# New timetables for three mixers, an early mean in the layer norms, and a block norm whose squares TensorE sums

## The reference

```
first block, twice:                                   # alpha = 4 ** 0.25
    x = layer_norm(alpha * x + 0.5 * swiglu_ffn(x))    # "ffn1", 2816 wide
    x = layer_norm(alpha * x + hybrid_mixer(x))        # "mixer"
    x = layer_norm(alpha * x + 0.5 * swiglu_ffn(x))    # "ffn2"
second block, with 16 meta tokens ahead of the 512:
    h = h + 0.5 * swiglu(rmsnorm(h))
    h = h + [diff_attention | top-k latent attention](rmsnorm(h) @ w_in) @ w_out
    h = h + 0.5 * swiglu(rmsnorm(h))
```

## Time and profile before

| | before |
|---|---|
| median of 3 runs | 3179.1 us |
| the profiled execution | 3178.52 us, span 3177.1 us |
| mean granted TensorE clock | 0.987 |
| PE busy | 3067.3 us, 97% |
| DVE busy | 1416.9 us, 45% |
| ACT busy | 1179.3 us, 37% |
| POOL busy | 372.4 us, 12% |
| DMA queues | 26% of 16 engines' span, 269.62 MB |

### The profile page before, as it was taken

One profiled execution on the slowest core, in us unless ns is written; L12 is line 12 of the kernel. 1 busy time (PEld: TensorE's weight loads), 2 busy tenths in 40 slices (PEclk: granted clock), 3 DMA queues, 4 the chain that ended last, 5 costly groups with the idle time before them and its releaser, 6 DMA issues.

```text
span 3177.1 us, 39372 instructions
## 1 busy us (share of the span) xinstructions
PE 3067.3 (97%) x16470; PEld 2564.3 (81%) x16470; DVE 1416.9 (45%) x2118; ACT 1179.3 (37%) x1914; POOL 372.4 (12%) x275
## 2 busy tenths in 40 slices
PE   9999999999999999999999999999999789799999
PEld 7888876888888888886788888899998657688888
DVE  3332455643335333375573333644323666554432
ACT  3322366433214222265552222522223456442321
POOL 0000133300001000033310001100014122110000
PEclk9999999999999999999999999999999899899999
DMA  4223221232232323331222233222233101122232
GB/s 157 93 92 92 97 87 54 67 107 93 91 97 78 107 93 89 97 108 54 67 81 99 93 91 95 69 91 91 84 93 108 34 27 41 34 87 93 98 88 80
DMA packets 76496, 269.62 MB, mean 85 GB/s; under 512 B 8720, under 2 KB 9008, under 8 KB 76064
## 3 DMA queue, kind: packets, MB, share of 16 engines
q1 hardware_dynamic: 74448, 260.08, 25.4%
q0 software_dynamic: 1872, 7.04, 0.7%
HBM read 264.97 MB, written 2.11 MB: 84 GB/s over the span
## 4 chain that ended last, share of the span: by engine, by line
PE 88%; DVE 6%; ACT 4%; issue 1%; DMA 0%; POOL 0%; SPq 0%; DVEq 0%; ACTq 0%
PE psum L339 25%; PE psum L342 24%; PE psum L345 24%; PE psum L400 3%; PE psum L412 2%; PE psum L362 1%; PE psum L358 1%; PE psum L360 1%; PE psum L636 1%; ACT w_hi L284 1%; DVE x_lo L703 1%; PE psum L2599 1%; DVE b_rank L2874 1%; ACT prob L1729 0%; DVE x L788 0%
## 5 line engine op out<-in xcount | busy, mean ns | idle before, releaser
L295 DVE TENSOR_TENSOR w_lo<-w_raw,w_hi 128x1024 fp32r<-128x1024 f32 (+1 forms) x442 | 551.5, 1250 | 1246.7 <-ACT w_hi L284 1246.6
L339 PE MATMUL psum<-x_hi,w_hi 128*128 128x512 f32 (+1 forms) x2792 | 967.9, 371 | 8.6 <-ACT neg_mean L2670 5.2
L342 PE MATMUL psum<-x_hi,w_lo 128*128 128x512 f32 (+1 forms) x2792 | 951.1, 365 | 0.0
L345 PE MATMUL psum<-x_lo,w_hi 128*128 128x512 f32 (+1 forms) x2792 | 946.3, 363 | 0.0
L284 ACT CAST w_hi<-w_raw 128x1024 fp32r<-128x1024 f32 (+1 forms) x490 | 504.0, 1029 | 1170.9 <-PE psum L345 1134.3
L339 PEld LDWEIGHTS psum<-x_hi,w_hi 128*128 128x128 f32 x2792 | 503.2, 190 | 114.2 <-issue 16.8
L342 PEld LDWEIGHTS psum<-x_hi,w_lo 128*128 128x128 f32 x2792 | 502.4, 190 | 87.7 <-issue 5.7
L345 PEld LDWEIGHTS psum<-x_lo,w_hi 128*128 128x128 f32 x2792 | 503.0, 190 | 84.4
L339 PE MATMUL psum<-h_hi_ffn,w_hi 128*128 128x512 f32 (+1 forms) x792 | 296.9, 375 | 0.0
L342 PE MATMUL psum<-h_hi_ffn,w_lo 128*128 128x512 f32 (+1 forms) x792 | 292.2, 369 | 0.0
L345 PE MATMUL psum<-h_lo_ffn,w_hi 128*128 128x512 f32 (+1 forms) x792 | 290.7, 367 | 0.0
(11 more groups left out here) (384 smaller groups left out, 3440.9 us busy)
## 6 DMA issues: line engine op xcount, KB each, us to landing
w_raw<-in_ffn_gu SPq DMA_DIRECT2D x176, 512.0 KB, 3.2
w_raw<-in_ffn_down SPq DMA_DIRECT2D x64, 512.0 KB, 3.5
w_raw<-in_w_in SPq DMA_DIRECT2D x44, 512.0 KB, 3.3
w_raw<-in_b_gate SPq DMA_DIRECT2D x44, 512.0 KB, 3.2
w_raw<-in_b_up SPq DMA_DIRECT2D x44, 512.0 KB, 3.3
w_raw<-in_b_down SPq DMA_DIRECT2D x32, 512.0 KB, 3.5
w_raw<-in_ffn_down SPq DMA_DIRECT2D x32, 384.0 KB, 3.1
w_raw<-in_b_in SPq DMA_DIRECT2D x24, 512.0 KB, 3.3
```

The lines of the kernel that those rows point to most:

```text
L295: nc.vector.tensor_tensor(w_lo[s][:, 0:n], w_raw[r][:, 0:n], w_hi[s][:, 0:n].bitcast(F32), ALU.subtract).then_inc(*w_low_dve.inc(u))
L339: nc.tensor.matmul(out, w_h, hi[:, c], start=first and i == 0, stop=False)
L342: nc.tensor.matmul(out, w_l, hi[:, c], start=False, stop=False)
L345: done = nc.tensor.matmul(out, w_h, lo[:, c], start=False, stop=final and i == n - 1)
```

## The change

- The start times and lags of the mixers' steps become tables (`TIMES_1`, `LAGS_1`, `TIMES_2`, `LAGS_2`), with other values. Steps hang on a start by a lag, as before. A lag can be negative.
- The mean that a layer norm shifts by is now that of two feature tiles of the old `x` (0 and 1), scaled. POOL adds the two (`pool_pair`), TensorE sums over features (`pe_mean`), ACT negates, and DVE makes x = scale * x - mean for all 8 tiles (`dve_shift`). In a feed-forward stage this happens at up-steps 20 (TensorE), 22 (ACT) and 24 to 38 (DVE); in a mixer at 19.9 to 24.3. The results of the product are then added without a scale. In the feed-forward norm POOL sums 7 tiles instead of 6, ACT squares each tile as it comes, and the sums and squares on POOL take turns.
- In the block norm TensorE sums the squares, one sum for each tile and part (`pe_square`), in three rotating buffers; POOL has no part in it. `x_hi` is made at once from the scaled tile, with the bias folded in (`shift2`), before `x` itself. The meta tokens' part (`act_meta`, `dve_meta`, 8 small matmuls) moves into the feed-forward stage before. The mean is copied to SBUF, and `dve_centre` reads it there.
- Small moves: `MixNorm`'s sums of part 1 one step later in `pe_group`, two weight splits on ACT earlier.

```diff
-EARLY = 6
 OUT_PAIRS = KT // 2
+
+
+
+TIMES_1 = {'turned': [0.38, 0, 0, 0.65, 0, 0.01, 0.1, 0, 0.07, 0.57, 0.36, 0.69, 0.17],
+ 'v_made': [2.53, 0.62, 0.26, 0.86, 1.58],
+ 'items': [6.34, 7.06, 8.68, 9.66, 12.97, 13.72, 16.16, 17.1],
+ 'retention': [9.28, 12.43, 15.67, 18.77],
+ 'r_high': 25.22,
+ 'mean': 20.2,
+ 'shift': [20.35, 20.57, 21.18, 21.19, 21.38, 23.27, 23.68, 24.26]}
+LAGS_1 = {'turned': [('swap', 0.41), ('cosine', 0.42), ('sine', 0.45), ('turned', 0.77)],
+ 'value': [('v_raw', -0.09), ('v_turn', 0.46)],
+ 'item': [('score', -0.02), ('mask', -0.0), ('exp', 0.56), ('denom', 1.15), ('prob', 1.22),
+          ('turn', 2.24), ('p_made', 2.56), ('value', 3.0), ('y_high', 3.06), ('y_low', 3.17)],
+ 'retention': [('weighted', 0.78), ('r_score', 0.87), ('k_turn', 0.88), ('k_made', 0.89),
+               ('decay', 0.9), ('r_kv', 1.08), ('state', 1.09), ('r_out', 1.63), ('o_made', 2.05),
+               ('r_sum', 2.1), ('o_centred', 2.28), ('o_square', 2.33), ('r_stat', 2.73),
+               ('o_root', 2.88), ('o_inverse', 2.89), ('o_norm', 2.94)],
+ 'mean': [('pair', -0.31), ('mean', -0.14), ('negate', 0.05)]}
+TIMES_2 = {'a': [9.64, 10.49, 11.1, 12.3, 12.63, 13.42, 14.35, 14.75, 21.6, 21.84, 22.63, 23.45, 24.58,
+       24.86, 25.79, 26.12],
+ 'b': [16.73, 17.1, 17.51, 17.88, 18.26, 18.59, 19.11, 19.28, 19.91, 20.33, 20.76, 21.05, 21.42,
+       21.85, 22.31, 23.13],
+ 'dots': [5.75, 5.9, 6.3, 6.48, 7.97, 8.08, 9.01, 9.12, 12.01, 12.23, 12.89, 13.07, 16.86, 17.03,
+          17.65, 17.74],
+ 'rounds': [(7.25, 0.102), (9.76, 0.281), (14.36, 0.31), (18.22, 0.265)],
+ 'window': [1.92, 3.15, 4.2, 5.32],
+ 'v_b': [1.22, 1.54, 1.93, 2.03, 2.17],
+ 'lat': [0.33, 0.45],
+ 'o': [3.55, 1.19, 1.42, 1.31],
+ 'a_y': [24.97, 24.49, 23.19, 25.69],
+ 'b_y': [23.81, 23.83, 23.83, 24.25],
+ 'first': 25.03}
+LAGS_2 = {'q_i': [('q_i', -0.39)],
+ 'k_i': [('k_i', 0.35)],
+ 'w_i': [('w_raw', -0.4), ('w_turn', -0.09), ('w_made', -0.08)],
+ 'q': [('q_square', -0.02), ('q_stat', 0.21), ('q_root', 0.35), ('q_inverse', 0.36)],
+ 'k': [('k_square', -0.21), ('k_stat', 0.58), ('k_root', 0.59), ('k_norm', 0.84)],
+ 'v': [('v_raw', 0.15), ('v_turn', 0.22), ('v_made', 0.23)],
+ 'c': [('c_add', 0.26), ('c_stat', 0.84), ('c_root', 0.85), ('c_norm', 1.02)],
+ 'v_b': [('v_b', 0.29), ('v_b_made', 0.48)],
+ 'qb': [('qb_raw', -0.18), ('lat_add', 0.64), ('lat_stat', 0.7), ('lat_root', 0.82),
+        ('lat_inverse', 0.86)],
+ 'lat': [('lat', -0.16), ('lat_square', 0.08)],
+ 'window': [('flip', -0.8), ('window', -0.27)],
+ 'dots': [('dots', 0.03), ('relu', 0.09), ('accumulate', 0.16)],
+ 'a': [('a_score', 0.07), ('a_bias', 0.09), ('a_exp', 0.39), ('a_mix', 0.49), ('a_turn', 0.79),
+       ('a_copy', 0.84), ('a_value', 1.04), ('a_out', 1.12)],
+ 'a_y': [('a_y_turn', 0.44), ('a_y_high', 0.54), ('a_y_low', 0.73)],
+ 'b': [('b_score', -0.04), ('b_mask', 0.06), ('b_bias', 0.12), ('b_top', 0.37), ('b_exp', 0.5),
+       ('b_turn', 0.7), ('b_inverse', 0.71), ('b_copy', 0.82), ('b_value', 1.01),
+       ('b_out', 1.02)],
+ 'b_y': [('b_y_turn', 0.03), ('b_y_high', 0.15), ('b_y_low', 0.16)]}
...
+                    if leave.first_mean and i == 20:
+                        leave.pe_first_mean()
...
+                    if leave.before_block and s == 12:
+                        leave.act_meta()
+                    if leave.first_mean and s == 22:
+                        leave.act_first_mean()
...
+                    if leave.before_block and s == 15:
+                        leave.dve_meta()
+                    if leave.first_mean and 24 <= s < 24 + 2 * KT and s % 2 == 0:
+                        leave.dve_shift((s - 24) // 2)
...
+            def pool_pair(self):
+                pool.wait_ge(*self.x_before(0))
+                pool.wait_ge(*self.x_before(1))
+                nc.gpsimd.tensor_tensor(neg_mean[:, TOK], x[:, 0, TOK], x[:, 1, TOK],
+                                        ALU.add).then_inc(*self.paired.inc(0))
+
+            def pe_mean(self, out):
+                pe.wait_ge(*self.paired.at(0))
+                nc.tensor.matmul(out, ones[:], neg_mean[:, TOK], start=True,
+                                 stop=True).then_inc(*self.mean_summed.inc(0))
+
+            def act_negate(self, product):
+                act.wait_ge(*self.mean_summed.at(0))
+                nc.scalar.mul(neg_mean[:, TOK], product,
+                              -self.scale / (2 * P)).then_inc(*self.negated.inc(0))
+
+            def dve_shift(self, m):
+                dve.wait_ge(*self.negated.at(0))
+                dve.wait_ge(*self.x_before(m))
+                if m < 2:
+                    dve.wait_ge(*self.paired.at(0))
+                nc.vector.scalar_tensor_tensor(
+                    x[:, m, TOK], x[:, m, TOK], self.scale, neg_mean[:, TOK],
+                    ALU.mult, ALU.add).then_inc(*self.shifted.inc(m))
...
+            def pe_begin(self):
+                pe.wait_ge(*self.first.meta_low.at(KT - 1))
+
+            def pe_square(self, k, part):
+                if k == 0:
+                    pe.wait_ge(*self.first.mean_copied.at(part))
+                pe.wait_ge(*self.first.sq2.at((k, part)))
+                done = self.first.pe_sum(256, self.squares[k % 3], part, k == 0, k == KT - 1)
+                done.then_inc(*self.first.sq2_summed.inc((k, part)))
+
+            def pe_within(self, part, step):
+
+                if (part, step) == (0, 1):
                     self.first.pe_late(1)
-                if (part, k) == (1, 9):
-                    self.first.pe_rms(0)
-                if (part, k) == (2, 0):
-                    self.first.pe_rms(1)
+                k = step if step < 2 else step - 2
+                if part < 2 and step not in (2, 3):
+                    if k:
+                        self.pe_square(k - 1, part)
+                    elif part:
+                        self.pe_square(KT - 1, 0)
+                if (part, step) == (2, 0):
+                    self.pe_square(KT - 1, 1)
+
...
+            def dve_centre(self, k, part):
+                c = self.cols[part]
+                dve.wait_ge(*self.inverse.at(part))
+                dve.wait_ge(*self.mean_copied.at(part))
+                nc.vector.tensor_tensor(x[:, k, c], x[:, k, c], neg_mean[:, c],
+                                        ALU.add).then_inc(*self.centred.inc((k, part)))
 
             def act_out(self, k, part):
 
-                c, full = self.cols[part], self.spread(part)
+                c, second = self.cols[part], self.second
                 act.wait_ge(*self.scaled.at((k, part)))
+                nc.scalar.activation(x_hi[:, k, c], x[:, k, c], ACT.Identity,
+                                     bias=shift2[:, k:k + 1], scale=gain(second.g, k)).then_inc(
+                                         *second.high.inc((k, part)))
                 nc.scalar.activation(x[:, k, c], x[:, k, c], ACT.Identity,
                                      bias=gain(self.b, k)).then_inc(*self.moved.inc((k, part)))
+                if k >= 3:
+                    act.wait_ge(*self.sq2_summed.at((k - 3, part)))
                 act.wait_ge(*self.moved.at((k, part)))
-                nc.scalar.mul(x_hi[:, k, full], x[:, k, full], gain(self.second.g, k)).then_inc(
-                    *self.second.high.inc((k, part)))
-                if k >= 3:
-                    act.wait_ge(*self.total2.at((k - 2, part)))
-                nc.scalar.activation((square[k % 2] if k else sq_sum)[:, full], x[:, k, full],
+                nc.scalar.activation(second.squares[k % 3][:, c], x[:, k, c],
                                      ACT.Square).then_inc(*self.sq2.inc((k, part)))
 
...
             def end_dve(self):
-                for m in range(2):
-                    self.dve_shift(m)
                 for m in range(KT):
-                    if m + 2 < KT:
-                        self.dve_shift(m + 2)
+                    self.dve_second(m, 0)
                     if m == 1:
                         dve_split(self.u_second + OUT_PAIRS - 1)
-                    self.dve_second(m, 0)
                 dve_split(self.u_next)
                 self.dve_second(0, 1)
...
-            item_start = [6.2, 7.1, 8.0, 9.2, 11.0, 13.0, 15.2, 17.3]
...
             wide = lambda tile: tile in kind and kind[tile][0] in wide_kinds
             ended = lambda tile: GROUP + 0.04 * tile if tile < GROUP else tile + 1.0
             a_items = [(h, b) for h in range(A_HEADS) for b in range(NB)]
-            a_start = [9.7, 10.7, 11.7, 12.7, 13.2, 13.9, 14.6, 15.3,
-                       21.6, 22.2, 22.8, 23.4, 24.55, 25.15, 25.8, 26.45]
+            a_start, dots_at, rounds_at = TIMES_2["a"], TIMES_2["dots"], TIMES_2["rounds"]
             b_items = [(b, h) for h in range(B_HEADS) for b in range(3)] + \
                 [(3, h) for h in range(B_HEADS)]
-            b_start = [16.4 + 0.4 * i for i in range(12)] + [21.2 + 0.5 * i for i in range(4)]
-            dots_at = [6.5, 9.0, 12.2, 16.0]
```

(25 more changed lines are left out.)

324 lines of the change are left out of this document (138 added, 186 removed).

## The result

The changed kernel takes 3132.01 us (median of 4 runs, 3129.83 to 3134.31) against 3178.89 for the one before beside it. The ratio is 0.9852, with a 95% interval of 0.9839 to 0.9864; the forecast was 3131. The profiled execution took 3134.31 us with a span of 3132.6, 44.5 less than before.

A forecast was written before the change was run, and what follows sets the result against it. TensorE, busy 3067.3 of 3177.1 us, was taken as the bound, so only its stalls and low-clock stretches could give time. Last mixer -37, first two -10, block norm -1: -48 on 3178.5, forecast 3131, range 3092 to 3169.

The forecast's parts named there:

- The last mixer's lists: Last mixer: new step order ends TensorE's stalls and clock dips; -20 us net idle, -17 clock, sum -37, bounds +8 and -75.
- The new waits: Last mixer: waits that the new list creates elsewhere, between 0 and 31 us, taken as 7.
- +4 for the uncovered 12 steps: Last mixer's end: `b_turn` 15 to `a_y_turn` 1 run with no product to cover them; costs 0 to 8 us, taken as 4.
- leaves 2: Last mixer's tail: waits of 3.3 us at `a_turn` 14 and 2.9 at `b_turn` 15, with `first` 3 put between, leave 2.
- the clock's part: Last mixer: of 23 us lost to the lowered clock about 17 go, as dips follow the long waits that vanish.
- The first two mixers: First two mixers' new lists: 3.2 us of waits and 1.8 of clock go, 5 each, 10 for two; bounds 0 and 26.
- The shifts: End of the first two mixers: moving eight shifts off VectorE's last stretch gains 0 us; the 4.8 us wait stays.
- The block norm: Block norm: squares summed on TensorE, GpSimd's adds gone; -1 us in the sum, bounds -3 and +7.
- The 14 sums: Block norm: 14 more sums on TensorE, 6.0 us, all but about 1 us covered; if nothing were, +6.0.
- The stalls move: Rival, last mixer: VectorE becomes the bound in the dense stretch and the dips stay; -20 us, 3159, chance 0.19.
- Slower: Rival, last mixer: early `k_square` and `qb_raw` steps hold up ScalarE and long waits return; +10 us, 3189, chance 0.07.
- the sign that I gave for it: Last mixer: it decides where ScalarE's idle time in front of the early steps exceeds a quarter of product, 1.39 us.

The follow-up runs named there:

- ksq_late: The kernel after, with the four k_square steps back from -0.21 to +0.03 of a tile behind their product; 3136.70 us, ratio 0.9865.
- early_mean_only: The kernel before with the early mean of two feature tiles alone, old lists and old block norm; 3181.26 us, ratio 1.0006.
- late_banks: The kernel after, with the first group behind a mixer using banks 3, 4, 5, 2, 0, a later bank wait and sums moved; 3122.43 us, ratio 0.9818.
- old_norm: The changed kernel with the block norm as before: GpSimd adds, two sums on TensorE, meta tokens inside the norm; 3128.03 us, ratio 0.9844.
- stats_early: The kernel after, with c_stat at 0.80 instead of 0.84 and k_stat at 0.51 instead of 0.58 of a tile; 3138.99 us, ratio 0.9873.

## Why the prediction was right, step by step

**The last mixer's lists: right in sum (-37, measured -37.9), by two errors that cancel.** I had -20 of idle and -17 of clock; it was -28.0 and -9.9.
- The mechanism holds. `k_square` 1 was to leave 1.3 us and left 1.2; `ksq_late` brings 3.5 back by one number. The waits of `q_stat` 1 (4.0), `a_turn` 6 (3.6) and `lat` 1 (5.0) no longer show. Waits for the relu (L2819) do: four of 1.1 or 1.2 us. The new waits were put at 7 us; the three for `a_bias` are 8.6.
- Too small was the gain in idle time. The term that failed is "+4 for the uncovered 12 steps" together with "leaves 2" for the tail. The last 80 us of before had 10.5 us idle; the last 71 of after have 5.0:

```profile
2726.00:2806.20 80.20, 69.65 (x441) 59.10 (x441) 41.56 (x87) 42.51 (x100) 20.75 (x17) 0.96 0.10 34
```

```profile
2690.00:2761.30 71.30, 66.35 (x407) 55.90 (x405) 36.57 (x83) 38.06 (x89) 20.78 (x17) 0.95 0.11 38
```

  By my terms this stretch would have gone up to some 13 us (10.5, less the 3.3 at `a_turn` 14, plus 2, plus 4). That it fell to 5.0 is as much as the whole 8 us by which the idle sum was off. The wait that I named as the test, over 3 us between `b_turn` 15 and `first` 0, is not there; the longest after 2690 is 1.5. TensorE's waits among the steps without product, from 2689 to 2697, are 0.9, 0.3, 0.5 and 0.3 us: they have one another to cover them. The other terms were off too, up and down, and their errors about cancel; I had not followed the small waits one by one.
- Too large was the clock's part. I took 17 of 23 us, because the dips (stretches at 1.2 GHz) would go with the long waits. But short waits in a row lower it as well: the clock is 0.95 in the tail of after, where no wait is over 1.5 us. It is at 0.51 from 2718.5 to 2725.3, and the waits before and at its start are 1.46 and 0.71 us.

**The first two mixers: a little low.** -5 each was the term. The stages lost 6.9 and 7.6, of which 1.6 or more came back in the stage behind; undoing the lists costs 10.5 us in the median and 13.5 up to the block norm, against the 10 of the term. The new list made a wait that I had not named, 2.5 us at the fourth item's score.

**The shifts: right.** 0 us was forecast, against the 4.8 that lie there. `early_mean_only` shows it at 1.0006 with the wait at 4.8, and the wait in the kernel after is still 4.85 us. VectorE's queue ahead of it had looked like the limit; what TensorE waited for was the banks that VectorE's last sums free, and `late_banks` removes this without giving VectorE less to do.

**The block norm: wrong in sign, inside its bounds.** -1 was the term, and by the stages of `old_norm` it is about +2 (+1.5 in the stage ahead, +0.6 in its own), less than the medians' intervals can tell from 0.
- The meta matmuls were put at 0 to 1 us and take 1.7, that is 0.106 us for each of 16 passes. A sum of 256 columns takes 0.43 in two passes, 0.215 each: with a sixteenth of the columns a pass costs half as much.
- The 14 sums were to be covered but for 1 us. TensorE's idle time in the stage fell by 1.0 only (7.9 to 6.9), while its passes rose by 27. That the stage still is but 0.6 longer comes from the clock. Its first 30 us before, after, and in `old_norm`:

```profile
1996.60:2026.60 30.00, 24.86 (x135) 20.88 (x136) 25.93 (x50) 22.74 (x53) 11.27 (x14) 0.89 0.06 18
```

```profile
1989.00:2019.00 30.00, 25.84 (x155) 21.91 (x156) 23.12 (x50) 23.17 (x53) 0.00 (x0) 1.00 0.05 19
```

```profile
1988.10:2018.10 30.00, 25.36 (x134) 21.73 (x135) 25.79 (x50) 22.56 (x52) 11.30 (x14) 0.83 0.05 18
```

  The clock is 1.00 in place of 0.89: 20 more passes in the same time. With the old norm it falls to 0.83 again. So most of the cover came from the clock, which I had not put into this term at all.
- GpSimd's 11.3 us are gone here, and VectorE does its work in 23.1 us instead of 25.9. The term took this from one split, 1.75 us beside an add. Five splits in the first 40 us averaged 1.31 us and now 1.21, which is 0.5 us in all. More comes from the 15 scalings of `x`, which the term had not named. Before, then after:

```profile
L795 DVE SCALAR_TENSOR_TENSOR x<-x,gains,z_sum 128x256 f32<-128x256 f32 x15 | 8.8, 588 | 0.0
L295 DVE TENSOR_TENSOR w_lo<-w_raw,w_hi 128x1024 fp32r<-128x1024 f32 x5 | 6.4, 1314 | 1.6 <-ACT w_hi L284 1.6
```

```profile
L891 DVE SCALAR_TENSOR_TENSOR x<-x,gains,z_sum 128x256 f32<-128x256 f32 x15 | 7.2, 478 | 0.0
L348 DVE TENSOR_TENSOR w_lo<-w_raw,w_hi 128x1024 fp32r<-128x1024 f32 x5 | 5.9, 1208 | 1.7 <-ACT w_hi L337 1.7
```

  `old_norm`, with the adds back, has 587 and 1313 ns for these two. This agrees with the rule of the Trainium skill, "SBUF — State Buffer", "Who interferes with whom", that a VectorE instruction with two SBUF inputs contends with a GpSimd instruction that reads SBUF. The edit that the rule speaks against did no harm here, where GpSimd does nothing: `dve_centre` takes 414 ns from two SBUF tiles and took 413 from PSUM. So the 2 us of VectorE came as summed; they bought TensorE at most the 1.0 above.

**The stages behind the mixers** were to be unchanged within 1 us. They were 1.6 and 3.9 longer. Of the 3.9, 1.7 are the meta matmuls. The low clock behind the mixer's last wait is another part: before it held for 3.4 and 2.8 us of these stages (from 627.9 and 1621.8 on), now for 5.1 and 5.7. At half speed that is 0.9 and 1.4 us. The 0.7 and 0.8 that are left I can't place. In the kernel after, from 619.3 on:

```profile
619.30:626.10 6.80, 5.13 (x20) 4.88 (x21) 3.84 (x10) 2.12 (x5) 0.62 (x1) 0.51 0.00 0
```

**The rivals.** "The stalls move" has a point: there are three new waits for `a_bias`, and in `stats_early` the one change tried against them only moved them. But VectorE isn't the bound. Over 2463 to 2590, which answers to the first of rows 3, it works 92 of 127 us, a share of 0.72 against 0.69 before, while TensorE's idle time there is 14.5 in place of 30.7. "Slower" did not come, but the sign that I gave for it did not decide either. ScalarE stands 0.95 us in front of `k_square` 1, but 4.24 in front of `k_square` 0, well over the quarter of 1.39. Behind it stood a weight split, and TensorE has no wait over 0.9 us from there to 2470. In front of the other six early steps it stands 1.36 us or less.

## What to carry to other kernels

Look for the long stall behind one in-order queue, and move the single step that stands behind work which itself waits. A negative lag costs nothing where no other engine is waiting for what stands behind the step. A bank that must be freed is a deadline too: change which bank is needed first before you make the engine that frees it faster. When you compare edits one by one, compare the stages that they touch, and don't add up what the others do.
